# Two places instead of three for weight blocks, three kept query blocks instead of two, in a one-core kernel of a hybrid block

## The chip, the cores and the metric

The kernel runs on one core of a Trainium2 chip. A core has TensorE (PE, matmuls; PEld is its weight load), VectorE (DVE), ScalarE (ACT), GpSimd (POOL) and SyncE (SP), which each run a program of their own in order and meet at semaphores, and 16 DMA engines that move data between HBM and the on-chip memory. The metric is the time of one execution on the device, in microseconds; less is better. A measurement of this kernel tells about 0.2% (3.5 us) from no change.

## The reference

Two layers over 256 tokens of width 1024, in float32. Each layer adds three things to `x`: a mixer (causal convolution, stick-breaking attention and a diagonal state-space model side by side, then `w_out`), cross attention over 256 memory rows (`w_mq`, `w_mkv`, `w_mo`), and a feed-forward layer (PEER) in which each token picks 16 of 16384 experts for each of 8 heads:

```python
def one_chunk(xc):                                   # 128 tokens
    q = (xc @ w_q).reshape(PEER_CHUNK, PEER_HEADS, 2, PEER_HALF)
    sc = jnp.einsum('chid,hikd->chik', q, sub_keys)
    top_s, top_i = lax.top_k(sc, PEER_TOPK)
    cand = (top_s[:, :, 0, :, None] + top_s[:, :, 1, None, :]).reshape(...)
    best_s, best_c = lax.top_k(cand, PEER_TOPK)
    i1 = jnp.take_along_axis(top_i[:, :, 0], best_c // PEER_TOPK, axis=-1)
    i2 = jnp.take_along_axis(top_i[:, :, 1], best_c % PEER_TOPK, axis=-1)
    gate = jax.nn.softmax(best_s, axis=-1)
    u_e, v_e = u_tab[i1 * PEER_KEYS + i2], v_tab[i1 * PEER_KEYS + i2]
    act = jax.nn.gelu(jnp.einsum('chkd,cd->chk', u_e, xc))
    return jnp.einsum('chk,chkd->cd', gate * act, v_e)
```

The gathers of `u_e` and `v_e` are the bulk of the bytes: 2 layers x 256 tokens x 128 experts x 8 KB = 537 MB.

## The kernel before, in words

**Chunks.** The 256 tokens are two chunks of 128; with two layers there are four chunks in turn, 0 to 3 (`ci`; chunks 0 and 1 are layer 0). For each chunk the kernel computes mixer, memory attention and PEER queries; the PEER gathers of a chunk run beside the mixer and the memory attention of the next.

**Gathers.** The 512 gathers (`NG`) each bring the row pair `u_e`, `v_e` of one expert per token, 128 x 2048 floats or 1 MB, into one of nine tiles `slots` (POOL, L962). VectorE forms the dot product with the token (`dot_of`, L1774), ACT the gelu (L1315), VectorE the coefficient, and then either TensorE adds the row through a diagonal matrix (`add_expert`, L851; ACT writes the diagonal, L1302) or VectorE adds it to `x` (`add_slot`); `TAKER` says who. Then the slot is free and POOL issues the gather nine further on.

**Weight blocks.** All weights come in blocks of 1 MB (128 x 2048 floats). Their names (`LIN`): `u`, `val`, `gate`, `q`, `k`, `v` for the mixer; `mk` and `mv`, four each, once a layer for the memory's keys and values; `out`, `mq`, `mo`, four each; `wq`, eight, one for each head of the PEER queries. SP issues the loads (L918) in the order in which TensorE takes the blocks (`take`). `place` says where a block lies: places 0 to 2 are the tile `ring`; places 3 to 9 are slots 2 to 8, used for weights only until the gathers need them (the first `EARLY` = 35 blocks go round all `WIDE` = 10 places, shifted by `AHEAD` = 5); after that blocks go round the three ring places. Places 10 and 11 are the tile `kept`: the first two of a layer's eight `wq` blocks stay there from the first chunk of the layer to the second, which therefore loads only six. The last two are the scratch tiles `W_` and `pr_`, for `u` and `val` of chunk 1. A load waits until the block that lay in its place before is used (`lain`, `free_at`). The first gather into a slot waits for the last block that lay in it.

**Order of the work.** Each engine's program is written out by a clock of ticks: one tick is one gather from tick 100 (`G0`) on. A piece of work (a strand) yields the tick at which its next part stands in the program; within an engine all is in that fixed order, and whatever waits holds up what stands behind it. `WQ_AT` are the ticks of the `wq` blocks, `KEYS_AT` those of the quarters of `mk` and `mv` blocks (3 ticks a block in layer 1), `MIX_AT` those of the halves of the mixer's nine blocks. In layer 1 the `mv` blocks end where chunk 2's mixer begins, so for three ticks both strands use blocks in turn.

**The first gathers.** The route of head 0 of chunk 0 (`routes`, VectorE) gives the first eight experts' indices before the rest. Its softmax is started by ACT in `gates`, at tick 98; the engine has one table of functions loaded at a time, so an `Exp` after a `Sqrt`, or a `Gelu` after an `Exp`, is preceded by a table load (ACT_TABLE_LOAD).

Of the kernel before, what the change touches and what calls it, by code (L numbers as in the profile page):

```python
# [11 lines left out]
ACT = mybir.ActivationFunctionType  # L12
# [19 lines left out]
PH, NK, TOP = 8, 128, 16  # L32
# [20 lines left out]
NPRM = _at  # L53
NVEC = PRM["b"][0]

RING = 3

EARLY = 35
WIDE = 10

AHEAD = 5

STAY = 2
SLOTS = 9
DIAGS = 4
WARM = 3
# [68 lines left out]
def build(nc, x_d, mem_d, blocks_d, prm_d, rows_d, experts_d, out_d):  # L135
    ctx = ExitStack()
    with ctx:
# [207 lines left out]

        def place(ci, what):

            if 0 <= what - FIRST["wq"] < STAY:
                return WIDE + what - FIRST["wq"]
            if ci == 1 and what < 2:  # L350
                return WIDE + STAY + what
            r = sum(p < WIDE for p, _ in spots)
            return (r + AHEAD) % WIDE if r < EARLY else (r - EARLY) % RING

        def lain(j):

            p, n = spots[j]
            return spots.index((p, n - 1)) if n else None

        def home(p):  # L360
            if p < RING:
                return ring[:, p, :]
            if p < WIDE:
                return slots[:, p - RING + 2, :]
            if p < WIDE + STAY:
                return kept[:, p - WIDE, :]
            return (W_, pr_)[p - WIDE - STAY][:, 0:KT * BW]

# [559 lines left out]
        @block.gpsimd  # L928
        def _(eng):
            nc.gpsimd.memset(epsb[:, :], EPS).then_inc(const_ok, 1)  # L930
            nc.gpsimd.memset(onec[:, :], 1.0).then_inc(const_ok, 1)
            nc.gpsimd.memset(zero[:, :], 0.0).then_inc(const_ok, 1)
            nc.gpsimd.memset(ident[:, :], 0.0).then_inc(const_ok, 1)
            nc.gpsimd.memset(ident16[:, :], 0.0).then_inc(const_ok, 1)
            nc.gpsimd.memset(mask[:, :], 0.0).then_inc(const_ok, 1)
            nc.gpsimd.iota(times[:, :], pattern=[[1, TP]], base=0, channel_multiplier=0,
                           allow_small_or_imprecise_dtypes=True).then_inc(const_ok, 1)
            nc.gpsimd.iota(iota16[:, :], pattern=[[1, TOP]], base=0, channel_multiplier=0,
                           allow_small_or_imprecise_dtypes=True).then_inc(const_ok, 1)
            eng.wait_ge(const_ok, 8)  # L940
            nc.gpsimd.affine_select(out=ident16[:, :], in_=ident16[:, :], compare_op=ALU.not_equal, fill=1.0,
                                    base=0, pattern=[[-1, P]], channel_multiplier=1).then_inc(const_ok, 1)
            nc.gpsimd.affine_select(out=ident[:, :], in_=ident[:, :], compare_op=ALU.not_equal, fill=1.0,
                                    base=0, pattern=[[-1, P]], channel_multiplier=1).then_inc(const_ok, 1)
            nc.gpsimd.affine_select(out=mask[:, :], in_=mask[:, :], compare_op=ALU.is_gt, fill=-BIG,
                                    base=0, pattern=[[-1, P]], channel_multiplier=1).then_inc(const_ok, 1)
            for n in range(NG):
                q, k = divmod(n, TOP)

                if k == 0:  # L950
                    eng.wait_ge(idx_ready, q + 2 if q else 1)
                elif n == 8:
                    eng.wait_ge(idx_ready, 2)
                if n >= SLOTS:
                    before = n - SLOTS
                elif n >= 2:

                    done, count = free_at[max(j for j in range(len(order)) if spots[j][0] == RING + n - 2)]
                    eng.wait_ge(done, count)
                if n >= SLOTS:  # L960
                    eng.wait_ge(slot_used if TAKER[before] == "tensor" else slot_added, TAKEN[before] + 1)
                nc.gpsimd.indirect_dma_start(  # L962
                    slots[:, n % SLOTS, :], None, experts_d,
                    bass.IndirectOffsetOnAxis(ap=idx[q % 2][:, k:k + 1], axis=0),
                ).then_inc(arrived[n % SLOTS], 16)

        @block.scalar
        def _(eng):
# [202 lines left out]
            def feed(ci):  # L1171
# [10 lines left out]
                if ci == 0:  # L1182
# [9 lines left out]
                    for i, part in enumerate("ab"):  # L1192
# [3 lines left out]
                        name = ("keys " + part, 0, 0)  # L1196
                        done(act(scores[:, 0, i * NK:(i + 1) * NK], full(name)[:, i * NK:(i + 1) * NK], ACT.Copy), name)
                    root_of_x(0, True)
                else:
                    for i in range(2):  # L1200
                        yield at + LATER[ci] + 88
# [66 lines left out]

            def gates():
                for q in range(NST * PH):  # L1270
                    yield route_tick(q, BEST_OP) + (1 if q else 4)
                    j = q % 2
                    eng.wait_ge(best_ready, q + 1)
                    if q < PH:
                        act(gexp[:, j, :], best[:, j, :], ACT.Exp, scale=rs0[:, :], bias=nbest[:, j, :],
                            accum_out=gsum[:, j, :]).then_inc(gexp_ready, 1)
                    else:
                        act(gexp[:, j, :], best[:, j, :], ACT.Exp, bias=nbest[:, j, :], accum_out=gsum[:, j, :])\
                            .then_inc(gexp_ready, 1)
# [661 lines left out]
```

## Time and profile before

| | |
|---|---|
| median of 3 runs | 1732.26 us (1731.23 to 1733.24) |
| the profiled execution | 1731.45 us, span 1729.5 us |
| granted TensorE clock | 0.987 of full speed, mean |
| PE busy | 1584.8 us (92%) |
| DVE busy | 1213.5 us (70%) |
| ACT, POOL busy | 601.3 us (35%), 589.0 us (34%) |
| DMA | 680.38 MB, mean 393 GB/s; gathers 536.90 MB, loads from SP 142.24 MB |
| chain that ended last | PE 35%, DMA 32%, DVE 13%, ACT 4% of the span |
| loads of weight blocks | ring 96, slots 26, kept 4, scratch tiles 2: 128 of 1 MB |

A busy PE is not PE at its peak, since ends of matmuls are modelled. Idle time of an engine costs nothing by itself; what counts is what the chain of waits passes through. An instruction's "releaser" is the one whose semaphore ended its wait.

### The profile page before, as it was taken

Reading aid. Unit: us, or ns where it says so; the run is one execution under the profiler, and the core shown is the slowest. Engines: PE = TensorE matmul, PEld = TensorE weight load, DVE = VectorE, ACT = ScalarE, POOL = GpSimd, SP = SyncE. Lnnn points to the kernel's source line nnn. Section 1 sums busy time; section 2 is a strip of 40 time slices with the busy share of each in tenths; the row PEclk is TensorE's granted clock in tenths of the full one; section 3 lists DMA queues with packets and bytes.
Section 4 is the critical chain, followed back from the end, with each engine's and each line's share of the span. In section 5 each row is a group of like instructions: output and inputs, shape, how many; then the busy total and the mean of one; then the engine's idle time right before and its main releaser. Section 6 shows DMA issues by size and latency. Waiting matters only on the chain.

```text
span 1729.5 us, 19577 instructions
## 1 busy us (share of the span) xinstructions
PE 1584.8 (92%) x6594; PEld 959.1 (55%) x6594; DVE 1213.5 (70%) x3359; ACT 601.3 (35%) x1450; POOL 589.0 (34%) x527
## 2 busy tenths in 40 slices
PE   8999989998999999998999989999999988777776
PEld 7877866445557776644646547644655643222232
DVE  7730689985896667997557567898657577667665
ACT  4133431553345132255223242255323223222222
POOL 0000153443334323344334343344333444333431
PEclk9999999999999999999999999999999999999999
DMA  9636799999999999999999999999999999999996
GB/s 383 245 150 239 292 392 421 421 405 421 421 407 412 421 421 420 420 421 421 421 422 420 421 419 421 419 368 402 422 421 421 421 421 421 421 421 421 420 421 258
DMA packets 94579, 680.38 MB, mean 393 GB/s; under 512 B 10488, under 2 KB 10768, under 8 KB 12304
## 3 DMA queue, kind: packets, MB, share of 16 engines
q0 software_dynamic: 73728, 536.90, 75.3%
q1 hardware_dynamic: 20752, 142.24, 20.2%
q8 instruction: 52, 0.85, 0.2%
q14 instruction: 47, 0.39, 0.1%
HBM read 678.06 MB, written 1.05 MB: 393 GB/s over the span
## 4 chain that ended last, share of the span: by engine, by line
PE 35%; DMA 32%; DVE 13%; ACT 4%; issue 2%; POOL 0%; DVEq 0%; ACTq 0%
DMA slots<-expert_rows,expert 32%; PE bank L851 20%; PE bank L408 7%; DVE slots L1774 5%; PE bank L586 2%; PE bank L839 2%; PE bank L836 2%; ACT diag L1302 1%; DVE sg L1341 1%; DVE htok L1625 1%; PE bank L453 1%; DVE coef L1341 1%; DVE x L1341 1%; DVE cands L1755 0%; ACT L1315 0%
## 5 line engine op out<-in xcount | busy, mean ns | idle before, releaser
L851 PE MATMUL bank<-slots,diag 128*128 128x512 f32 x1916 | 909.6, 611 | 128.9 <-ACT diag L1302 123.8
L962 POOL DMA_INDIRECT slots<-expert_rows,expert x512 | 587.0, 1147 | 1115.5 <-PE bank L851 856.7
L1774 DVE CUSTOM_DVE_ANT_0 slots<-slots,htok 128x1024 f32<-128x1024 f32 x512 | 626.6, 1224 | 336.6 <-DMA slots<-expert_rows,expert 323.5
L851 PEld LDWEIGHTS bank<-slots,diag 128*128 128x128 f32 x1916 | 348.6, 193 | 544.7 <-issue 324.2
L1315 ACT ACTIVATE gel<-dot 128x2 f32<-128x2 f32 (+1 forms) x258 | 52.5, 204 | 675.6 <-DVE dot L1774 674.8
L1302 ACT ACTIVATE diag<-ident,coef 128x128 f32<-128x128 f32 x479 | 168.2, 394 | 190.4 <-DVE coef L1341 181.8
L408 PEld LDWEIGHTS bank<-hT,ring 128*128 128x128 f32 x1632 | 198.6, 193 | 44.7 <-issue 44.4
L408 PE MATMUL bank<-hT,ring 128*128 128x128 f32 x1632 | 199.0, 276 | 0.0
L1341 DVE SCALAR_TENSOR_TENSOR coef<-gel,ginv,gexp 128x2 f32<-128x2 f32 (+1 forms) x258 | 55.1, 213 | 58.6 <-ACT gel L1315 57.1
L1315 ACT ACT_TABLE_LOAD x66 | 84.7, 1283 | 1.2
L1341 DVE SCALAR_TENSOR_TENSOR sg<-pad,prm,sg 128x128 f32<-128x128 f32 x240 | 71.7, 344 | 0.0
L408 PE MATMUL bank<-hT,slots 128*128 128x128 f32 x480 | 56.7, 276 | 3.7 <-DMA slots<-w_blocks 2.5
L408 PEld LDWEIGHTS bank<-hT,slots 128*128 128x128 f32 x480 | 55.2, 192 | 5.1 <-DMA slots<-w_blocks 2.7
L586 PE MATMUL bank<-ring,products 128*128 128x512 f32 x120 | 57.1, 603 | 0.0
L586 PE MATMUL bank<-ring,hT 128*128 128x512 f32 x112 | 52.3, 593 | 0.0
L1774 DVE DVE_READ_ACCUMULATOR2_ANT dot<- 128x1 f32 x512 | 42.3, 83 | 0.0
L1341 DVE SCALAR_TENSOR_TENSOR x<-slots,coef,x 128x1024 f32<-128x1024 f32 x33 | 42.2, 1280 | 0.0
L586 PEld LDWEIGHTS bank<-ring,products 128*128 128x128 f32 x120 | 23.0, 195 | 27.0 <-issue 26.9
L586 PEld LDWEIGHTS bank<-ring,hT 128*128 128x128 f32 x112 | 21.0, 190 | 23.8 <-issue 23.6
L839 PE MATMUL bank<-ring,w 128*128 128x256 f32 x128 | 29.3, 379 | 0.0
L836 PE MATMUL bank<-w,ring 128*128 128x256 f32 x128 | 29.1, 379 | 0.0
L408 PEld LDWEIGHTS bank<-hT,kept 128*128 128x128 f32 x208 | 25.2, 192 | 5.7 <-issue 5.7
(315 smaller groups left out, 1520.4 us busy)
## 6 DMA issues: line engine op xcount, KB each, us to landing
ring<-w_blocks SPq DMA_DIRECT2D x96, 1024.0 KB
slots<-w_blocks SPq DMA_DIRECT2D x26, 1024.0 KB, 7.2
slots<-expert_rows,expert POOLq DMA_INDIRECT x512
kept<-w_blocks SPq DMA_DIRECT2D x4, 1024.0 KB, 12.9
keys<-w_blocks SPq DMA_DIRECT2D x2, 1024.0 KB, 10.7
prm<-small SPq DMA_DIRECT2D x2, 768.0 KB
x<-x_rows SPq DMA_DIRECT2D x2, 512.0 KB, 11.6
slots<-mem_rows SPq DMA_DIRECT2D x1, 1024.0 KB, 9.1
```

The lines of the kernel that those rows point to most:

```text
L408: last = mm(bank[b][:, a * P:(a + 1) * P], w[:, k, a * P:(a + 1) * P], src[:, k, :], start=k == 0, stop=k == KT - 1)
L453: last = mm(bank[b][:, 0:BW], hT[:, k, :], w[:, k, :], start=k == 0, stop=k == KT - 1)
L586: last = mm(bank[b + i][:, :], src[:, first + k, :], w[:, k, i * 512:(i + 1) * 512], start=start and k == 0, stop=stop and k == 1)
L836: last = mm(bank[b][:, a * M:(a + 1) * M], w[:, k, a * P:(a + 1) * P], memH[l][:, k, :], start=k == 0, stop=k == KT - 1)
L839: last = mm(bank[b][:, a * BW:(a + 1) * BW], memH[l][:, k, a * P:(a + 1) * P], w[:, k, :], start=k == 0, stop=k == KT - 1)
L851: last = mm(bank[h][:, :], diag[:, i % DIAGS, :], slots[:, n % SLOTS, D + h * 512:D + (h + 1) * 512], start=m == 0, stop=n == end)
L962: nc.gpsimd.indirect_dma_start(slots[:, n % SLOTS, :], None, experts_d, bass.IndirectOffsetOnAxis(ap=idx[q % 2][:, k:k + 1], axis=0),).the ...
L1302: act(diag[:, i % DIAGS, :], ident[:, :], ACT.Copy, scale=coef[:, q % 2, k:k + 1])\
L1315: act(gel[:, q % 2, k:k + many], dot[:, q % 2, k:k + many], ACT.Gelu_apprx_tanh).then_inc(gelu_ready, 1)
L1341: return v.scalar_tensor_tensor(out=out, in0=in0, scalar=scalar, in1=in1, op0=op0, op1=op1)
L1625: did(v.tensor_tensor_scan(back(stay[:, h, lo:S]), back(sn[:, h, lo:S]), zero[:, :].to_broadcast([P, S - lo]), 1.0, ALU.mult, ALU.add))
L1774: v.tensor_tensor_reduce(out=slots[:, s, 0:D], in0=slots[:, s, 0:D], in1=htok[:, ph % 2, :], scale=1.0, scalar=0.0, op0=ALU.mult, op1=ALU.add,
```

## The change

The tile `ring` has two places instead of three and `kept` three instead of two, so both together take the same memory. The kept blocks are now the last three of a layer's `wq` blocks (heads 5 to 7) instead of the first two. The wide round has nine places, ring 0 and 1 and the seven slots, of which the first 34 blocks use; `slot_at` maps place 2 to slot 6, 3 to 7, 4 to 8, and 5 to 8 to slots 2 to 5. With the new `EARLY` and `AHEAD`, chunk 0's `wq` blocks 0 and 1 lie in the ring, 2 to 4 in slots 6 to 8, 5 to 7 in `kept`, and its four `mo` blocks in slots 2 to 5. Before, its `wq` blocks 0 and 1 lay in `kept` and 2 to 7 in slots 3 to 8, and its last `mo` block in slot 2. The second chunk of each layer loads five `wq` blocks instead of six: 126 loads instead of 128. Besides, ACT executes one more `Exp` of a zero in the opening, whose table load comes earlier, and the softmax of head 0 of chunk 0 stands at tick 94 of ACT's program instead of 98.

```diff
-RING = 3
+RING = 2
-EARLY = 35
-WIDE = 10
-AHEAD = 5
-STAY = 2
+EARLY = 34
+WIDE = 9
+AHEAD = 7
+STAY = 3
...
         def place(ci, what):
-            if 0 <= what - FIRST["wq"] < STAY:
-                return WIDE + what - FIRST["wq"]
+            if what >= FIRST["wq"] + PH - STAY:
+                return WIDE + what - (FIRST["wq"] + PH - STAY)
...
+        def slot_at(p):
+            return 2 + (p - RING + 4) % (WIDE - RING)
+
         def home(p):
             if p < RING:
                 return ring[:, p, :]
             if p < WIDE:
-                return slots[:, p - RING + 2, :]
+                return slots[:, slot_at(p), :]
...
-                    done, count = free_at[max(j for j in range(len(order)) if spots[j][0] == RING + n - 2)]
+                    done, count = free_at[max(j for j in range(len(order))
+                                              if RING <= spots[j][0] < WIDE and slot_at(spots[j][0]) == n)]
...
                     root_of_x(0, True)
+                    act(ahead[:, :], zero[:, :], ACT.Exp)
...
-                    yield route_tick(q, BEST_OP) + (1 if q else 4)
+                    yield route_tick(q, BEST_OP) + (1 if q else 0)
```

POOL's program at the first gathers (slots 0 to 8 in turn, then slot 0 again), before. `filled` and `pair_used` are TensorE's signals that a block has been used, `slot_used` and `slot_added` that an expert has been added, `idx_ready` that indices are there:

```order
L962 DMA slots<-expert_rows,expert 128x2048 [waits idx_ready]
L962 DMA slots<-expert_rows,expert 128x2048
L962 DMA slots<-expert_rows,expert 128x2048 [waits filled3] x2
L962 DMA slots<-expert_rows,expert 128x2048 [waits filled2]
L962 DMA slots<-expert_rows,expert 128x2048 [waits filled3]
L962 DMA slots<-expert_rows,expert 128x2048 [waits filled2]
L962 DMA slots<-expert_rows,expert 128x2048 [waits filled3]
L962 DMA slots<-expert_rows,expert 128x2048 [waits filled2,idx_ready]
L962 DMA slots<-expert_rows,expert 128x2048 [waits slot_used] x2
```

and now:

```order
L967 DMA slots<-expert_rows,expert 128x2048 [waits idx_ready]
L967 DMA slots<-expert_rows,expert 128x2048
L967 DMA slots<-expert_rows,expert 128x2048 [waits pair_used] x3
L967 DMA slots<-expert_rows,expert 128x2048 [waits filled3] x2
L967 DMA slots<-expert_rows,expert 128x2048 [waits filled2]
L967 DMA slots<-expert_rows,expert 128x2048 [waits filled3,idx_ready]
L967 DMA slots<-expert_rows,expert 128x2048 [waits slot_used] x2
L967 DMA slots<-expert_rows,expert 128x2048 [waits slot_added]
```

Slots 2 to 4 now wait for `mo` blocks (`pair_used`), slot 5 for the last of them, and slots 6 to 8 for `wq` blocks 2 to 4; before, six gathers waited for `wq` blocks 2 to 7.

ACT's program around the first softmax (`gexp`), before; `qT` holds the queries of a head, L1219 copies them out of a bank, L1210 the scores:

```order
L993 ACTIVATE root<-ss,epsb 128x1 [waits act_step]
L1219 ACTIVATE qT<-bank 128x256 [waits filled2]
L1210 ACTIVATE scores<-bank 128x256 [waits filled5]
L1219 ACTIVATE qT<-bank 128x256 [waits filled3]
L1210 ACTIVATE scores<-bank 128x256 [waits filled6]
L1219 ACTIVATE qT<-bank 128x256 [waits filled2]
L1275 ACT_TABLE_LOAD
L1275 ACTIVATE gexp,gsum<-best,nbest,rs 128x16 [waits best_ready]
L1210 ACTIVATE scores<-bank 128x256 [waits filled5]
L1219 ACTIVATE qT<-bank 128x256 [waits filled3]
```

and now:

```order
L998 ACTIVATE root<-ss,epsb 128x1 [waits act_step]
L1204 ACT_TABLE_LOAD
L1204 ACTIVATE ahead<-zero 128x1
L1225 ACTIVATE qT<-bank 128x256 [waits filled2]
L1281 ACTIVATE gexp,gsum<-best,nbest,rs 128x16 [waits best_ready]
L1216 ACTIVATE scores<-bank 128x256 [waits filled5]
L1225 ACTIVATE qT<-bank 128x256 [waits filled3]
L1216 ACTIVATE scores<-bank 128x256 [waits filled6]
L1225 ACTIVATE qT<-bank 128x256 [waits filled2]
L1216 ACTIVATE scores<-bank 128x256 [waits filled5]
```

The softmax stands behind one copy of queries instead of three, and its table load before the copy of head 1's queries; the first `gel` (not shown) has the same five copies of queries ahead of it in both.

TensorE's program where the last `mv` blocks (L839, now L843) and chunk 2's first blocks `u`, `val`, `gate` (L408, now L412) meet, before; `loaded0` to `loaded2` are the loads into the ring's places:

```order
L839 MATMUL bank<-ring,w 128x256 x4
L408 MATMUL bank<-hT,ring 128x128 [waits loaded2,emptied2,emptied5]
...
L839 MATMUL bank<-ring,w 128x256 [waits loaded0,emptied4]
L839 MATMUL bank<-ring,w 128x256 x7
...
L408 MATMUL bank<-hT,ring 128x128 x8
L839 MATMUL bank<-ring,w 128x256 x4
...
L408 MATMUL bank<-hT,ring 128x128 [waits loaded1,emptied3]
L408 MATMUL bank<-hT,ring 128x128 x7
L839 MATMUL bank<-ring,w 128x256 x4
L408 MATMUL bank<-hT,ring 128x128 x8
...
L408 MATMUL bank<-hT,ring 128x128 [waits loaded2,emptied2]
```

and now:

```order
L843 MATMUL bank<-ring,w 128x256 x4
L412 MATMUL bank<-hT,ring 128x128 [waits loaded1,emptied2,emptied5]
...
L843 MATMUL bank<-ring,w 128x256 [waits loaded0,emptied4]
L843 MATMUL bank<-ring,w 128x256 x7
...
L412 MATMUL bank<-hT,ring 128x128 x8
L843 MATMUL bank<-ring,w 128x256 x4
...
L412 MATMUL bank<-hT,ring 128x128 [waits loaded1,emptied3]
L412 MATMUL bank<-hT,ring 128x128 x7
L843 MATMUL bank<-ring,w 128x256 x4
L412 MATMUL bank<-hT,ring 128x128 x8
...
L412 MATMUL bank<-hT,ring 128x128 [waits loaded0,emptied2]
```

The instructions are the same and stand in the same order. What moved is the place: `u` waits for place 1 instead of 2, the last `mv` block for place 0, which the third `mv` block leaves in this piece's first row, `val` for place 1, which `u` leaves two instructions earlier, and `gate` for place 0, which the last `mv` block leaves between the halves of `val`.

## Rows read from the trace of the kernel before

**Rows 1.** Stages: span, busy us (instructions) of PE, PEld, DVE, ACT, POOL; PEclk, DMA share, GB/s

```profile
210.00:220.00 10.00, 8.81 (x57) 6.73 (x56) 6.61 (x15) 7.90 (x15) 2.96 (x4) 1.00 0.50 168
...
476.00:545.00 69.00, 66.14 (x307) 42.07 (x306) 52.02 (x142) 34.31 (x78) 24.55 (x21) 0.95 1.00 406
545.00:676.00 131.00, 131.00 (x650) 100.47 (x649) 90.09 (x223) 39.59 (x92) 45.97 (x39) 1.00 1.01 421
676.00:1120.00 444.00, 416.22 (x1725) 246.24 (x1724) 321.27 (x900) 149.42 (x371) 168.34 (x142) 0.98 1.01 420
1120.00:1200.00 80.00, 75.08 (x258) 36.69 (x257) 73.26 (x194) 46.28 (x92) 34.12 (x27) 1.00 0.98 381
1200.00:1690.00 490.00, 414.60 (x1310) 204.71 (x1309) 325.77 (x891) 143.75 (x381) 196.52 (x184) 0.99 1.01 421
```

**Rows 2.** Chain of waits around 664 us: start, us, what

```profile
663.88 20.35 DMA slots<-expert_rows,expert
```

**Rows 3.** Timeline of POOL, opening: start, us, engine, line, what, [idle before <-releaser]

```profile
188.74 1.09 POOL L962 DMA_INDIRECT slots<-expert_rows,expert  x1 [186.07 <-DVE expert L1341]
...
193.24 0.94 POOL L962 DMA_INDIRECT slots<-expert_rows,expert  x1 [0.82 <-PE bank L408]
...
200.32 0.94 POOL L962 DMA_INDIRECT slots<-expert_rows,expert  x1 [3.08 <-PE bank L408]
...
216.32 0.94 POOL L962 DMA_INDIRECT slots<-expert_rows,expert  x1 [6.18 <-PE bank L408]
```

**Rows 4.** Timeline of ACT, then VectorE, opening

```profile
196.47 1.28 ACT L1275 ACT_TABLE_LOAD   x1
197.76 0.40 ACT L1275 ACTIVATE gexp<-best,nbest,rs 128x16 f32<-128x16 f32 x1
...
198.35 0.16 DVE L1781 RECIPROCAL ginv<-gsum 128x1 f32<-128x1 f32 x1 [2.82 <-ACT gexp L1275]
...
206.04 0.22 DVE L1341 SCALAR_TENSOR_TENSOR coef<-gel,ginv,gexp 128x2 f32<-128x2 f32 x1 [3.30 <-ACT gel L1315]
```

**Rows 5.** Waits of VectorE 224 to 256, of TensorE 224 to 300: us, times, longest

```profile
DVE slots L1774 <- DMA slots<-expert_rows,expert: 3.5, 5, 1.0
...
PE bank L851 <- ACT diag L1302: 3.4, 2, 2.1
```

**Rows 6.** DMA issues of 164, 605 and 871 us: KB each, us from issue to landing

```profile
w<-w_blocks SPq DMA_DIRECT2D x1, 1024.0 KB, 4.8
...
keys<-w_blocks SPq DMA_DIRECT2D x1, 1024.0 KB, 14.5
...
kept<-w_blocks SPq DMA_DIRECT2D x2, 1024.0 KB, 16.1
```

**Rows 7.** Timeline of SP's queue around the stretch of mk and mv

```profile
605.06 0.33 SPq L918 DMA_DIRECT2D ring<-w_blocks  x1
...
615.40 0.33 SPq L918 DMA_DIRECT2D ring<-w_blocks  x1
```

**Rows 8.** Timeline of TensorE at the out blocks of chunk 1

```profile
371.66 3.60 PE L586 MATMUL bank<-ring,hT 128*128 128x512 f32 x8
...
380.25 1.88 PE L586 MATMUL bank<-ring,hT 128*128 128x512 f32 x4
```

**Rows 9.** Timeline of TensorE where mv's last blocks and chunk 2's first meet

```profile
635.95 1.89 PE L839 MATMUL bank<-ring,w 128*128 128x256 f32 x8
...
639.46 3.62 PE L839 MATMUL bank<-ring,w 128*128 128x256 f32 x16
...
644.63 1.95 PE L408 MATMUL bank<-hT,ring 128*128 128x128 f32 x16
...
649.86 1.95 PE L408 MATMUL bank<-hT,ring 128*128 128x128 f32 x16
651.64 1.89 PE L839 MATMUL bank<-ring,w 128*128 128x256 f32 x8
...
658.16 3.73 PE L408 MATMUL bank<-hT,ring 128*128 128x128 f32 x32
```

## The prediction

> **What bounds the kernel now.** I read the table of stages first. The DMA engines move 421, 420 and 421 GB/s from 545 to 676, 676 to 1120 and 1200 to 1690 us, but 406 from 476 to 545 and 381 from 1120 to 1200 [rows 1]. A block of weights and a gather are 1.05 MB each (128 rows of 8 KB), so each costs 1.05 / 421 = 2.49 us of that throughput. Two engines stand close behind: TensorE is busy 131.00 of 131.00 us from 545 to 676 us, and VectorE 73.26 of 80.00 us from 1120 to 1200 us [rows 1]. So DMA is full, but the end passes through DMA only where the engines have slack; elsewhere a megabyte saved becomes idle DMA.
>
> Then the chain of waits. It runs through TensorE's instructions up to 663.6 us and at 663.88 goes over to one gather that is 20.35 us from issue to landing [rows 2]: 8 MB stand in the queues, some 5 or 6 gathers and the weight blocks. That backlog is what a TensorE stall can eat before DMA goes idle.
>
> **The change part by part.** *The opening's gathers.* POOL issues the first gather at 188.74 us, and its fourth to ninth at 193.24 to 216.32 us, most held by query blocks that TensorE still reads in slots 3 to 8 (the ninth waits 6.18 us for the last of them); DMA falls to 168 GB/s between 210 and 220 us [rows 1, 3]. In the changed kernel slots 2 to 5 hold mo blocks, done before 177 us, slots 6 to 8 the third to fifth query blocks. At POOL's own spacing of 1.24 to 1.4 us six gathers go out by 195 us, and the ninth when the fifth query block is done: today that is what releases the sixth gather, 200.32 us [rows 3]. The ninth is 16 us earlier, and DMA, which needs 2.49 us for each, is some 7 us further by 225 us. Of this, 2.5 us go again, because chunk 1's fifth block can no longer be fetched before the gathers start. What the engines can make of the 5 us left is less. The first coefficients wait for ACT until 206.04 us, and ACT's place in its program is behind query blocks that TensorE computes until 208 us, so nothing before 206 moves [rows 4]. From 224 us on VectorE waits for gathers 3.5 us in all, five times, the longest 1.0 us, and TensorE for diagonals 3.4 us, in two waits of which the longest is 2.1 us, its only ones until 300 us [rows 5]. So the gain lies between 0 (the waits turn into others) and 5 us (DMA's whole lead). I take 3, what the rows of waits give.
>
> *The exp edits.* They take a table load of 1.28 us and the wait of 2.82 us out of VectorE's way at 198.35 us [rows 4]. VectorE today then waits 3.30 us for the first gelu, at 206.04, and that wait grows by what the other loses. I cost this at 0; the cover is ACT's order behind the query copies. If that cover were gone it would be worth up to 2.8 us. The Trainium skill, page "ScalarE: Activation LUTs", section "What ACT_TABLE_LOAD costs", puts a drain of 1380 ns behind the 1283 ns of the load. The trace disagrees on the drain: the exp starts 1.29 us after its load started [rows 4]. By the page the edit would free 2.66 us, still under the same cover.
>
> *Two blocks less to load.* Three kept query blocks instead of two save one load in the second chunk of each layer: 2 x 2.49 = 5.0 us of DMA. The first saving falls near 486 to 545 us, the stage in which DMA has idle time already (406 GB/s) and which TensorE, busy 66.14 of 69 and then 131 of 131, carries on [rows 1]: worth nearly nothing. The second falls into 1200 to 1690, where DMA is full; but with a ring of two each load is issued one block later, so one block more is still to come when this stage begins at about 1195 us, and 12 loads are issued in it then as now. Bounds 0 and 5.0 us, I take 1.
>
> *Ring of two: which blocks come late.* With two places a block is issued when the block before the last is done, and has to land while one block is used. What a load takes: 4.8 us with no gather under way; 14.5 us for the keys issued 0.8 us behind a weight block, so two megabytes among gathers; 16.1 us for the kept pair behind a third [rows 6]. A single one among gathers therefore needs between 4.8 and 14.5 us; I take 9 (estimate: half of 14.5 is 7.3, a third of 16.1 is 5.4, and both carry the gathers ahead of them once more). Going through all uses, the time from one block's end to the start of the next but one is over 10 us almost everywhere: in the mk and mv stretch loads leave 10.3 us apart [rows 7], so a block has 10.3 us plus the gap between two. It is less in these places:
> - The out block used fourth, in chunks 1, 2 and 3: the instructions from 371.66 to 375.26 us are the second out block's last half and the third's first, so the second ends at about 373.5, and the fourth is used at 380.25 [rows 8]: 6.8 us, short by 2.2. Three of these make 6.6 us of TensorE stall. At 380 us two weight blocks and three or more gathers are under way, over 10 us of DMA work, so little reaches the end: between 0 and 6.6, I take 1.
> - The seam of layer 1's mv blocks and chunk 2's u, where both strands use blocks at once. Mv's third block ends at 637.84 and its fourth starts at 639.46: gap 1.6. U ends at 646.58, val starts at 649.86: 3.3. The fourth mv block ends at 653.5, gate starts at 658.16: 4.6 [rows 9]. At 9 us each the stalls are 7.4, 5.7 and 4.4: 17.5 us in which TensorE, the busiest engine there, stands. While it stands, no add of experts frees a slot, gathers under way dwindle, and loads get quicker; with the second and third load at 7 us the sum is 7.4 + 3.7 + 2.4 = 13.5.
>
> What these 13.5 us cost: the gather that is issued at 663.88 today and lands at 684.2 [rows 2] is issued at 677.4 and then finds nearly empty queues. Alone it would need about 5 us, with the weight blocks asked for in the same moments 10: it lands at 682 to 687. So the end is between 0 (the backlog of 20.35 us swallows all) and 17.5 + 10 - 20.35 = 7.2 us later; I take 3.
>
> Everything queued behind a waiting TensorE instruction (adds, then slots, POOL's gathers, then VectorE's dot products) is in that account. On SP's queue chunk 2's kept loads now leave as three in a row with the fourth-to-last query load, a burst of 4 MB; DMA stays full and TensorE has 28 us of slack in that stage (416.22 of 444 [rows 1]), so 0. Opening blocks in nine instead of ten places: each is issued over 30 us before its use, 0.
>
> **The sum.** -3 (opening) - 0 (exp) - 1 (bytes) + 1 (out) + 3 (seam) = 0. The profiled execution took 1731.45 us with a span of 1729.5; the median of the runs is 1732.26, 0.8 above it. I forecast the same time, 1732.3.
>
> **Rivals.**
> - *A, faster: DMA decides throughout.* For it: 420 and 421 GB/s in stages that make up 1065 of the 1729.5 us [rows 1]. Then the lead of 5 us in the opening and the 5.0 us of the two blocks arrive whole, and the stalls vanish in the backlog: -5 - 5 + 1 = -9, 1723. Against it: TensorE's 131 of 131 us, and the two stages in which DMA idles. Half of it, -5 (1727), is what comes if only one of the savings arrives. Chance 0.31 for all that is faster by over 0.2%.
> - *B, slower: the seam stalls TensorE past the backlog.* One mechanism at one place, 637 to 680 us: the loads stay at 9 us or more, or the gathers' issue comes back later than I count. With 17.5 us of stall and a gather that needs 10 us after it, +7.2; with the opening at 0 to -3 the sum is +5 to +8, so 1737 to 1740. It decides from some 17 us of stall on: 17 + 10 - 20.35 = 6.6, and the other terms (-3 - 1 + 1) leave +3.6. Chance 0.25. The Trainium skill, page "DMA: Bandwidth & Descriptors", section "Queues, rings and completion order", says that each DMA engine takes turns between the queues that have work, a packet at a time. By that rule a weight block's landing does not get shorter until the gathers are all but gone, so the stalls would be the 17.5 us of B and not 13.5. The kept pair's 16.1 us for loads issued among gathers [rows 6] don't contradict it, and no row here shows a load with only one gather beside it.
> - *C, the change does not do what it says:* the earlier gathers bring nothing, since query blocks, ACT and VectorE set the pace until 254 us. Then +3 on my sum, 1735: still within 0.2%. It is part of the 0.44 for no change.
>
> **Chances and range.** 0.2% is 3.5 us, about what a measurement of this kernel tells from no change. My forecast with C: 0.44; A 0.31; B 0.25. The range of 8 in 10 reaches into A to 1725 (the half case and some) and into B to 1740. The forecast's own range is 1729 to 1735.5.
>
> **What would show it.** Opening: the ninth gather issued at about 200 us instead of 216.32, DMA above 300 GB/s between 210 and 220, VectorE's waits for gathers before 256 gone. The exp: no wait for gexp at 198 us, the first coefficients still at about 206 us. Ring: TensorE waiting for loads of weights at the fourth out block by 2 us and at the start of mv's last block, val and gate by 7, 4 and 2, nowhere else by more than 1; DMA's throughput between 640 and 690 below 421. Loads: 126 weight blocks instead of 128. I am wrong if the seam shows under 5 us or over 17 us of stall, if the shift at 300 us is not -1 to -5, or if the shift from 700 us to the end changes by more than 2.

## The result, and the profile after

The changed kernel takes 1741.47 us (median of 5 runs, 1738.5 to 1742.34) where the kernel before takes 1732.9 (1731.23 to 1733.44): the ratio is 1.0055, with a 95% interval of 1.0043 to 1.0067. That is slower, and outside the range of 1725 to 1740. The profiled execution took 1741.47 us with a span of 1739.5.

Of the page of the changed kernel these lines answer to the ones of before: the engines' busy shares, the granted clock and DMA's throughput in 40 slices, two groups on TensorE that now wait for weight blocks, and the loads.

```profile
span 1739.5 us, 19572 instructions
PE 1588.9 (91%) x6594; PEld 963.5 (55%) x6594; DVE 1211.6 (70%) x3359; ACT 601.3 (35%) x1451; POOL 580.6 (33%) x527
...
GB/s 385 216 149 262 295 368 422 409 411 411 421 421 420 421 395 295 421 421 421 421 421 421 421 421 420 421 385 399 417 421 421 421 421 422 421 421 422 421 421 275
...
L590 PE MATMUL bank<-ring,hT 128*128 128x512 f32 x96 | 49.2, 643 | 7.9 <-DMA ring<-w_blocks 7.9
...
L843 PE MATMUL bank<-ring,w 128*128 128x256 f32 x128 | 33.5, 418 | 7.6 <-DMA ring<-w_blocks 7.6
...
ring<-w_blocks SPq DMA_DIRECT2D x92, 1024.0 KB
slots<-w_blocks SPq DMA_DIRECT2D x26, 1024.0 KB, 6.8
...
kept<-w_blocks SPq DMA_DIRECT2D x6, 1024.0 KB, 12.4
```

The slices are 43.5 us long. The 16th, 652 to 696 us, moves 295 GB/s, the least between 218 us and the last slice, and the one ahead of it 395. The table of stages (columns as in [rows 1]) puts it more finely.

```profile
210.00:220.00 10.00, 10.00 (x69) 8.09 (x68) 8.08 (x23) 7.12 (x16) 2.18 (x3) 1.00 0.79 303
...
545.00:676.00 131.00, 120.14 (x541) 91.37 (x539) 74.85 (x176) 31.34 (x78) 36.72 (x32) 0.93 0.92 377
640.00:646.00 6.00, 0.39 (x4) 0.20 (x2) 4.85 (x13) 0.40 (x1) 0.00 (x0) 0.80 1.02 423
646.00:654.00 8.00, 5.98 (x15) 4.77 (x16) 0.05 (x1) 0.00 (x0) 0.00 (x0) 0.51 0.45 188
654.00:660.00 6.00, 6.00 (x32) 4.62 (x31) 0.00 (x0) 0.38 (x1) 0.94 (x1) 1.00 0.30 79
660.00:664.00 4.00, 1.52 (x4) 0.38 (x2) 0.00 (x0) 0.00 (x0) 1.88 (x2) 1.00 1.04 424
664.00:671.00 7.00, 6.25 (x23) 5.74 (x24) 0.00 (x0) 0.00 (x0) 0.00 (x0) 0.51 0.74 291
...
1200.00:1690.00 490.00, 416.85 (x1305) 205.39 (x1304) 330.30 (x909) 143.95 (x381) 195.97 (x184) 0.99 1.01 420
```

From 646 to 660 us DMA falls to 188 and 79 GB/s, VectorE does next to nothing until 671, and TensorE works at a granted clock of 0.51 in two of the stretches. TensorE's timeline there, against [rows 9]:

```profile
636.72 1.89 PE L843 MATMUL bank<-ring,w 128*128 128x256 f32 x8
638.44 1.95 PE L412 MATMUL bank<-hT,ring 128*128 128x128 f32 x16
648.02 6.56 PE L843 MATMUL bank<-ring,w 128*128 128x256 f32 x16 [7.63 <-DMA ring<-w_blocks]
654.42 1.88 PE L855 MATMUL bank<-slots,diag 128*128 128x512 f32 x4
656.13 1.95 PE L412 MATMUL bank<-hT,ring 128*128 128x128 f32 x16
...
664.75 3.75 PE L412 MATMUL bank<-hT,ring 128*128 128x128 f32 x16 [3.23 <-DMA ring<-w_blocks]
668.30 3.18 PE L843 MATMUL bank<-ring,w 128*128 128x256 f32 x8
671.32 1.95 PE L412 MATMUL bank<-hT,ring 128*128 128x128 f32 x16
...
676.42 3.81 PE L412 MATMUL bank<-hT,ring 128*128 128x128 f32 x32 [0.16 <-DMA ring<-w_blocks]
```

Gate's block starts at 676.42 instead of 658.16. Of these 18.3 us, 7.63 + 3.23 + 0.16 = 11.0 are waits. Another 6.0 are the same matmuls at half clock: 6.56 for 3.62, 3.75 for 1.95, 3.18 for 1.89. The chain of waits runs through exactly these pieces:

```profile
638.63 9.25 DMA ring<-w_blocks
...
648.02 6.56 PE bank L843 x16
...
658.11 6.51 DMA ring<-w_blocks
...
664.75 3.75 PE bank L412 x16
...
671.51 4.77 DMA ring<-w_blocks
```

Val's load is issued at 658.11, 19.5 us after the mv block's: it waits for the end of u, whose second half (656.13) stands behind the mv block on TensorE. With u ending at 646.58, as in [rows 9], it would have been 8.

What each engine waited for from 636 to 700 us (us in total, times, longest):

```profile
POOL slots L967 <- PE bank L855: 47.1, 9, 17.2
DVE coef L1347 <- ACT gel L1321: 26.2, 1, 26.2
ACT memV L1266 <- PE bank L843: 18.0, 2, 13.0
ACT uT L1033 <- PE bank L412: 17.4, 1, 17.4
```

This is how a wait on TensorE spreads: ScalarE stands 17.4 us at the copy of u and 13.0 at the copy of mv, the gelu behind them comes late, VectorE stands 26.2 us at one coefficient (longest before: 5.5), no slot is freed, and POOL issues no gather for 17.2 us.

To see where time goes over the whole run I compare the start of VectorE's dot product n (L1774, now L1780; the first is 0) in pairs of traces; dot product n needs gather n. Us later than in the trace of before:

```
n                  1    8    32    56    64    88   136   144   160   208   240   312   320   384   448
changed kernel   -1.7 +4.9 +0.9  +1.3  +5.7   0.0  -2.2 +17.9 +12.1 +11.8 +18.0 +11.8 +15.0 +10.1 +10.0
e_mv3_kept       -0.6 +4.1 +0.1  +0.5  +6.7  +2.1  +1.2  +5.6  +0.4  +0.4  +6.7  +0.5  +5.9  +0.6  +0.7
e_busy_short     -2.3 +0.1 -1.2  -0.8  +4.6  -1.3  -2.0 +12.2  +6.7  +5.9 +12.1  +5.9  +9.6  +4.6  +4.6
e_ring2_alone    +3.7 +3.7 +5.6  +4.3 +11.6  +5.4  +6.4 +22.7 +17.4 +16.1 +16.1 +16.1 +20.9 +18.2 +18.2
```

The last column is the end. The first gather itself is issued 1.0, 2.2, 0.1 and 3.7 us later than before in these traces, by how the first weight loads land within 20 us of the start; that offset has to be taken off before one reads a term. In the changed kernel all of the loss is made between 136 and 160 (+14.3); the steps at 64, 240 and 320 are given back. A trace is one execution and need not be its kernel's median: that of e_mv3_kept took 1732.24 us (median 1727.53), that of e_busy_short 1736.0 (1732.69) and that of e_ring2_alone 1749.76 (1747.1), each the slowest of its kernel's runs. So I read steps between two n from the traces, and totals from the medians.

### The profile page after: what moved, and what is told of

It reads as the page before. It is cut to its first block, busy times and chain, and to the rows that moved or that the text cites. A ratio compares the mean times of both kernels' runs of the same rounds, so it can differ in the third digit from the quotient of the medians.

```text
span 1739.5 us, 19572 instructions
## 1 busy us (share of the span) xinstructions
PE 1588.9 (91%) x6594; PEld 963.5 (55%) x6594; DVE 1211.6 (70%) x3359; ACT 601.3 (35%) x1451; POOL 580.6 (33%) x527
## 4 chain that ended last, share of the span: by engine, by line
PE 53%; DMA 29%; DVE 8%; issue 5%; ACT 4%; SPq 0%; POOL 0%; DVEq 0%
DMA slots<-expert_rows,expert 25%; PE bank L855 24%; PE bank L412 10%; PE bank L590 4%; DMA ring<-w_blocks 3%; PE bank L843 3%; DVE slots L1780 3%; PE bank L840 3%; PE bank L457 1%; PE bank L490 1%; ACT diag L1308 1%; PE bank L475 1%; DMA slots<-w_blocks 1%; PE bank L678 1%; PE bank L420 1%
## 5 line engine op out<-in xcount | busy, mean ns | idle before, releaser
L967 POOL DMA_INDIRECT slots<-expert_rows,expert x512 | 578.7, 1130 | 1133.9 <-PE bank L855 888.8
L1780 DVE CUSTOM_DVE_ANT_0 slots<-slots,htok 128x1024 f32<-128x1024 f32 x512 | 625.6, 1222 | 279.6 <-DMA slots<-expert_rows,expert 269.7
L412 PEld LDWEIGHTS bank<-hT,ring 128*128 128x128 f32 x1584 | 192.8, 193 | 48.8 <-issue 47.6
L412 PE MATMUL bank<-hT,ring 128*128 128x128 f32 x1584 | 194.3, 277 | 5.2 <-DMA ring<-w_blocks 4.4
L412 PEld LDWEIGHTS bank<-hT,kept 128*128 128x128 f32 x384 | 45.9, 192 | 8.1 <-issue 8.1
L412 PE MATMUL bank<-hT,slots 128*128 128x128 f32 x352 | 43.6, 281 | 6.2 <-DMA slots<-w_blocks 4.5
L412 PE MATMUL bank<-hT,kept 128*128 128x128 f32 x384 | 46.3, 275 | 0.0
L412 PEld LDWEIGHTS bank<-hT,slots 128*128 128x128 f32 x352 | 42.1, 197 | 7.3 <-issue 3.7
L590 PE MATMUL bank<-ring,products 128*128 128x512 f32 x96 | 45.1, 592 | 0.0
L1780 DVE DVE_READ_ACCUMULATOR2_ANT dot<- 128x1 f32 x512 | 41.8, 82 | 0.0
L843 PE MATMUL bank<-ring,w 128*128 128x256 f32 x128 | 33.5, 418 | 7.6 <-DMA ring<-w_blocks 7.6
L843 PEld LDWEIGHTS bank<-ring,w 128*128 128x128 f32 x128 | 27.0, 214 | 14.7 <-issue 10.7
## 6 DMA issues: line engine op xcount, KB each, us to landing
keys<-w_blocks SPq DMA_DIRECT2D x2, 1024.0 KB, 11.8
```

Of the source, the lines that this page charges most:

```text
L412: last = mm(bank[b][:, a * P:(a + 1) * P], w[:, k, a * P:(a + 1) * P], src[:, k, :], start=k == 0, stop=k == KT - 1)
L590: last = mm(bank[b + i][:, :], src[:, first + k, :], w[:, k, i * 512:(i + 1) * 512], start=start and k == 0, stop=stop and k == 1)
L843: last = mm(bank[b][:, a * BW:(a + 1) * BW], memH[l][:, k, a * P:(a + 1) * P], w[:, k, :], start=k == 0, stop=k == KT - 1)
L967: nc.gpsimd.indirect_dma_start(slots[:, n % SLOTS, :], None, experts_d, bass.IndirectOffsetOnAxis(ap=idx[q % 2][:, k:k + 1], axis=0),).the ...
L1780: v.tensor_tensor_reduce(out=slots[:, s, 0:D], in0=slots[:, s, 0:D], in1=htok[:, ph % 2, :], scale=1.0, scalar=0.0, op0=ALU.mult, op1=ALU.add,
```

## The experiments

Each was timed beside the kernel before, on the same chip. The times are medians; the ratio to before, given with its 95% interval, is not the quotient of the two medians.

**e_ring2_alone: the ring of two and nothing else.** The kernel before with

```diff
-RING = 3
+RING = 2
...
-WIDE = 10
-
-AHEAD = 5
+WIDE = 9
+
+AHEAD = 1
```

> The kernel before with a ring of two places and nothing else of the change: two kept query blocks, the opening's query blocks in slots 3 to 8, exp and gates as before. Theory (the seam): the whole loss is made where layer 1's last mv block, val and gate are waited for, about 14 us between VectorE's 136th and 160th dot product, and the bytes saved by the third kept block gave about 4 us of it back in the changed kernel. So this one should be slower than the changed kernel: 1732.9 + 14 = 1747 us (1745 to 1749). Rival (the bytes are worth nothing, as the prediction had it at 1 us, and part of the loss comes from the opening or the out blocks): 1741 to 1743 us. In the profile the theory wants TensorE waits of 7 to 8 us and 3 us for ring blocks at 640 to 665 us, and the granted clock at its lower level behind them.

Measured: 1747.1 us against 1732.73, ratio 1.0074 (1.0057 to 1.009). TensorE's waits for weight blocks in it:

```profile
PE bank L586 <- DMA ring<-w_blocks: 9.6, 3, 4.1
PE bank L839 <- DMA ring<-w_blocks: 7.4, 1, 7.4
PE bank L408 <- DMA ring<-w_blocks: 5.3, 3, 3.1
...
PE bank L836 <- DMA ring<-w_blocks: 2.8, 1, 2.8
```

The time is as the theory had it, and the rest of the change is worth 5.6 us of gain. The clock is not as the theory had it: in the seam it falls behind the first wait alone, and for a shorter time.

```profile
656.50 5.93 PE L839 MATMUL bank<-ring,w 128*128 128x256 f32 x16 [7.43 <-DMA ring<-w_blocks]
...
672.49 2.02 PE L408 MATMUL bank<-hT,ring 128*128 128x128 f32 x16 [3.11 <-DMA ring<-w_blocks]
```

That is 2.4 us of half clock instead of 6.0, and the step between dot products 136 and 160 is 11.0 us instead of 14.3. A mk block (L836) waits too, which no mk block does in the changed kernel. Of the other 7.2 us at the end of this trace 3.7 are there from the start and 2.5 come between n = 376 and 384, of which more below (e_ring2_mv3).

**e_mv3_kept: one block out of the ring.** The changed kernel with, in `place`,

```diff
+            if ci == 2 and what == FIRST["mv"] + 3:
+                return WIDE
```

> The changed kernel with one block moved out of the ring: layer 1's last mv block goes into a kept place, which is empty between chunk 1's and chunk 2's query blocks. Theory: one wait starts it all. Val's and gate's waits follow from the first, since u's second half stands behind the mv block on TensorE and the loads of val and gate wait for u and mv; with it all three go, the clock stays up, and the time is 1741.5 - 14 = 1727.5 us (1726.5 to 1729), 0.3% below the kernel before. Rival (each of the three waits stands by itself, as the prediction summed them): val's and gate's waits of 3 to 4 us each stay and the time is 1732 to 1737 us.

Measured: 1727.53 us, ratio 0.9964 (0.9951 to 0.9977): the 14 us go, and the kernel is faster than before. In the traces the step between 136 and 160 goes from +14.3 to -0.8. TensorE there:

```profile
644.96 3.69 PE L845 MATMUL bank<-kept,w 128*128 128x256 f32 x16 [1.14 <-DMA kept<-w_blocks]
...
655.44 1.95 PE L414 MATMUL bank<-hT,ring 128*128 128x128 f32 x16
```

Val (655.44) no longer waits: its load goes out when the third mv block is done, and gate's when u is. So the three waits were one chain with one start. Moving one block is enough.

**e_busy_wait and e_busy_short: the same waits, with TensorE busy.** The changed kernel with matmuls whose result is overwritten, ahead of the wait for the mv block and for val:

```diff
+            def idle_turns(b, many):
+                for _ in range(many):
+                    mm(bank[b][:, 0:BW], ident[:, :], T[:, 0, :, 0:P], start=True, stop=True)
...
+                                if (kind, i, l) == ("mv", 3, 1):
+                                    idle_turns(b, 34)
...
+                    if (n, ci) == (1, 2):
+                        idle_turns(b, 14)
```

> The changed kernel with matmuls whose result nobody reads placed on TensorE ahead of the two waits: 34 of 128x256 ahead of the last mv block (about 7.3 us) and 14 ahead of val (about 3.0 us). The loads come when they come, so the waits are no shorter, but TensorE is busy in them. Theory: of the 18 us by which TensorE is late at gate's block, 6 us are matmuls at the granted clock of 0.5 behind the two waits (the mv block took 6.56 us instead of 3.62, val's first half 3.75 instead of 1.95, the next mv half-block 3.18 instead of 1.89). With the clock kept up 6 us go, and at the end 4 to 6 us: 1735.5 to 1737.5 us. Rival (the clock does not matter there, because DMA or VectorE sets the pace, or the fall has another cause): 1741 to 1743 us.

Measured: 1745.6 us, ratio 1.0081 (1.0067 to 1.0096). A miss: one matmul of this kind stands as two instructions in the trace, and I had taken the duration of one instruction for that of a matmul.

```profile
639.95 14.84 PE L410 MATMUL bank<-phasor,ident 128*128 128x256 f32 x68
654.63 3.62 PE L852 MATMUL bank<-ring,w 128*128 128x256 f32 x16
```

The filling is 7.2 + 3.0 us longer than the waits, but the mv block takes 3.62 us again. The second try has `idle_turns(b, 17)` and `idle_turns(b, 7)`.

> The changed kernel with half of the matmuls of the try before: 17 ahead of the last mv block (68 pieces took 14.84 us there, so these take 7.4 us, the length of the wait) and 7 ahead of val (3.1 us). Theory (half clock costs 6 us of the 18): the try before was too long by 7.2 + 3.0 us and ran 4.1 us longer than the changed kernel, which is 10.2 less the 6 us of the clock. With the right length 4 to 6 us go: 1735.5 to 1737.5 us. Rival (the clock does not matter, and the try before only lost less than its length): 1741 to 1743 us.

Measured: 1732.69 us against 1732.74, ratio 1.0001 (0.9992 to 1.001): 8.8 us less than the changed kernel, more than the 4 to 6 expected.

```profile
640.49 7.50 PE L410 MATMUL bank<-phasor,ident 128*128 128x256 f32 x34
648.35 3.72 PE L852 MATMUL bank<-ring,w 128*128 128x256 f32 x16 [0.35 <-DMA ring<-w_blocks]
...
671.02 3.81 PE L417 MATMUL bank<-hT,ring 128*128 128x128 f32 x32 [0.46 <-DMA ring<-w_blocks]
```

The mv block still cannot start before 648.35, and nothing else of the change was touched, yet gate starts at 671.02 instead of 676.42, with the granted clock at 1.00 throughout. Between dot products 136 and 160 this kernel loses 8.7 us and the changed one 14.3. So 5.6 us of the seam is the half clock; e_ring2_alone fits, with 3.6 us less of half clock on TensorE and 3.3 us less of loss. The medians are 8.8 us apart and the two profiled executions 5.5. Where the other 3.2 us of the medians lie no trace shows: the seam may cost more in other executions, or the opening (this trace lacks the stop told below and starts its gathers 0.9 us earlier).

**e_opening: the opening alone.** The kernel before (ring of three, exp as before) with the last two query blocks kept and

```diff
+            if 29 <= r < EARLY:
+                return (0, 1, 7, 8, 9, 2)[r - 29]
```

and `AHEAD = 8`, so that slots 2 to 5 are free early.

> The kernel before with the changed kernel's opening alone: ring of three, two kept blocks, but these are the last two, and the third to fifth query blocks stand in slots 6 to 8, the others in the ring, so that slots 2 to 5 are free for gathers early. Exp and gates as before. The prediction on record gives this -3 us (1730), from gathers that come earlier. Theory now: the first coefficients wait for ScalarE and TensorE, dot products 2 to 9 are no earlier, and by 300 us the shift is 0: 1732 to 1734 us. A third way: the stop of 2.3 us that TensorE shows at 197.5 us in the changed kernel, while nine gathers are asked for at once, belongs to this opening; then a stop of 2 to 3 us shows here at 195 to 200 us too, and dot products 2 to 9 are 3 to 5 us later than before.

Measured: 1729.06 us, ratio 0.9981 (0.9972 to 0.999), so -3.7: the prediction on record was right here, and my theory after the result wrong. I had read the trace of the changed kernel at n = 8 (+4.9), where a stop of TensorE hides the gain; that stop shows here too.

**e_exp_alone: the two edits for exp, in the kernel before.**

```diff
+                    act(ahead[:, :], zero[:, :], ACT.Exp)
...
-                    yield route_tick(q, BEST_OP) + (1 if q else 4)
+                    yield route_tick(q, BEST_OP) + (1 if q else 0)
```

> The kernel before with the two edits for exp alone (the function is called up early, and the first exp's tick is 4 less). The prediction on record and the theory: 0, since the first coefficients wait for ScalarE's order behind the query copies: 1732 to 1734 us. Rival: the earlier exp saves up to 2.8 us on VectorE, 1730.

Measured: 1731.33 us against 1732.74, ratio 0.9997 (0.9988 to 1.0006). No difference that can be told. The wait moves as predicted: the one for gexp is gone, and

```profile
204.77 0.22 DVE L1342 SCALAR_TENSOR_TENSOR coef<-gel,ginv,gexp 128x2 f32<-128x2 f32 x1 [6.02 <-ACT gel L1316]
```

the one for the first gelu has grown from 3.30 to 6.02 us, at the old place (this trace runs 1.3 us ahead from its first loads on).

**e_mv3_reload3: what a load costs.** e_mv3_kept, in which `take` loads the three kept query blocks again for the second chunk of each layer (`and c` becomes `and c > 1`).

> The changed kernel with the mv block in a kept place (1727.5 us), in which the three kept query blocks are loaded again for the second chunk of each layer, into the same places: 132 loads instead of 126, six times 1.05 MB, 15 us of DMA. Nothing else moves. The prediction on record takes 1 us of 5.0 for two loads saved, so 3 us of 15: 1730 to 1731 us. Theory now (a kernel with a ring of two and two kept blocks ran 5.6 us longer than the changed kernel, of which the opening is 3.7, so two loads are worth about 2): 6 us, 1733 to 1734. Rival (each megabyte arrives whole): 15 us, 1742.

Measured: 1739.53 us, ratio 1.0046 (1.0032 to 1.0059): 12.0 us for six loads, 2.0 each. Against e_mv3_kept its dot products go from 1.8 us earlier at n = 352 to 5.6 later at n = 376, where the second layer's three loads lie and DMA moves 421 GB/s: 7.4 us, three times 2.49 whole. Both my theory (6) and the prediction (3, by its 1 of 5.0) were low; the rival, each megabyte whole (15), was nearer.

**e_mv3_spaced: the gathers of the opening spread out.** e_mv3_kept with, on POOL,

```diff
+                    if n == 5:
+                        done, count = free_at[order.index((0, FIRST["wq"] + 3))]
+                        eng.wait_ge(done, count)
```

> The changed kernel with the mv block in a kept place, whose sixth gather waits until the fourth query block is done (about 198.5 us) instead of leaving at 197: five gathers are on their way instead of seven when TensorE came to its stop of about 2 us at 197 to 200 us in all four kernels that ask for nine gathers at once. DMA still has work for 12 us. If the stop comes from the heap of gathers, it is gone or shorter in the profile, dot products 2 to 9 are 2 us earlier against the first gather, and the time is 0 to 2 us less than 1727.5. If it comes from something else at that place of the program (code that is fetched then, say), it is still there at the same matmuls.

Measured: 1726.62 us, ratio 0.9969 (0.9959 to 0.998). TensorE's stop is not in its trace, but the median is only 0.9 below e_mv3_kept, which the measurement does not tell from nothing.

**e_ring2_mv3: the ring of two without its seam.** e_ring2_alone with the same two lines in `place`.

> The kernel before with a ring of two (as the run with the ring of two alone, 1747.1 us), and layer 1's last mv block in a kept place. Opening, kept query blocks and exp as before, 128 loads. Theory: outside the seam a ring of two costs next to nothing, since the waits of 2.5 to 3 us at the fourth out block of three chunks are made up by the gathers on their way; so this is the kernel before again, 1732 to 1735 us. Rival (the out blocks cost what they wait, 6 to 9 us in all, as the upper bound of the prediction had it): 1739 to 1742.

Measured: 1735.34 us against 1733.03, ratio 1.0014 (1.0005 to 1.0023), just above the 1735 of the theory. So outside the seam two places cost 2.3 us. Against e_ring2_alone the one block is worth 11.8 us here (1747.1 less 1735.34) where it was worth 14.0 in the changed kernel. Its trace waits 8.6 us for the three fourth out blocks and gives those back; it loses 2.5 us between n = 376 and 384. The last weight block is asked for at 1376.7 us instead of 1363.5, and so lies among gathers that had DMA for themselves; from 1200 us on this kernel asks for 13 weight blocks, the kernel before for 12.

**e_seam_all_kept: val and gate in kept places too** (`if ci == 2 and 1 <= what < 3: return WIDE + what`, on e_mv3_spaced).

> The kernel with the mv block in a kept place and the sixth gather held back (1726.6 us), with val and gate of chunk 2 in kept places too, so that no block of the seam waits for the ring. TensorE still waits 1.4 us for the mv block and 1.4 us in two waits for val and gate there. Theory: these short waits are made up by the gathers on their way, so nothing is left: 1725.5 to 1727.5 us. Rival (they reach the end): 1724 us.

Measured: 1726.22 us, ratio 0.9966 (0.9952 to 0.998): as the theory had it, and not to be told from e_mv3_spaced or e_mv3_kept.

## Why the prediction was wrong

The sum on record was -3 - 0 - 1 + 1 + 3 = 0. The runs price its terms like this:

- *Opening, -3.* Right: -3.7 (e_opening). DMA moves 303 GB/s from 210 to 220 us instead of 168, and VectorE's waits for gathers before 256 us are gone, as forecast. The shift I wanted to see at 300 us (-1 to -5) did not show in the changed kernel's trace (+0.9 at n = 32, of which 1.0 is the start). The stop of TensorE told below may be a part of that, but is not shown to be all of it: less the start, the shift at n = 32 is -0.1 (changed), -0.6 (e_busy_wait), -2.1 (e_mv3_kept) and -3.1 (e_opening) in traces with the stop, and -1.3 (e_busy_short) and -3.9 (e_mv3_reload3) without. The ninth gather is issued at 205.70 us and not at 200, and at 200.92 in e_busy_short, which has no stop; the first coefficients stand at 210.91 and not at 206.
- *Exp, 0.* Right in time and in mechanism (e_exp_alone).
- *Two loads less, -1.* Mis-sized: about -4 by the price of a load in e_mv3_reload3 (two of six in 12.0 us). The step that failed is that the first saving is "worth nearly nothing". The changed kernel goes from +0.8 at n = 104 to -2.2 at n = 136 (524 to 630 us in the kernel before), and so, by 2.9 to 3.0 us, do all six kernels with two places and three blocks that stay kept; e_ring2_alone and e_ring2_mv3, with two kept blocks, move by +0.3 and +0.2. The step on the second saving, "12 loads are issued in it then as now", held: from 1200 us on e_mv3_kept asks for 12 weight blocks as the kernel before does, and e_ring2_mv3, whose ring of two is not made up by a kept block, for 13, which costs it 2.5 us. So the -4 here and the +2.3 of the next point hold that one load with opposite signs.
- *Out blocks, +1.* Right in mechanism: the wait of TensorE at the fourth out block is 7.9 us in three waits (2.2 each were forecast), and n = 64 and 320 show steps that are gone at 88 and 384. The half clock is here too: the four matmuls behind these waits take 3.61, 2.99 and 3.56 us in the changed kernel, against 1.88 for four at full clock. The burst of kept loads in chunk 2, priced at 0, shows the same way at n = 240 (+18.0) and is gone at 312. With what else two places cost it is +2.3 (e_ring2_mv3).
- *Seam, +3.* This is what failed: 14.0 us (1741.47 less 1727.53). The waits were foreseen well and in sum a little too high (7.4, 3.7 and 2.4 against 7.63, 3.23 and 0.16), and the first load too (9 us against 9.25). Two things were not in the account. First, a TensorE that waits 7.63 us comes back at half clock: 6.0 us more on TensorE, of which 5.6 reach VectorE's dot product 160 (e_busy_short). Second, "the backlog of 20.35 us swallows": this step of the prediction took one gather's time from issue to landing, at 664 us, as cover for the whole. In the trace POOL ends one gather's issue at 639.3 us and the next at 657.5, and DMA moves nothing from 653 to 658 us, so that a single gather (issued at 656.57) is ahead of the next wait. The stop of the gathers is 18 us and not 7.6, because the adds that free slots wait for VectorE and ScalarE, and ScalarE stands in its order behind the copies of u and mv. Without the clock the 11.0 us of waits still cost 8.7; the backlog covered 2.3. The price of the seam is 14.0 us in the changed kernel and 11.8 in the one with the ring of two alone.

The terms priced so give -3.7 - 1.4 - 4 + 2.3 + 14 = +7.2 (with the exp edits at their median, which is no difference that can be told), or +5.0 with the seam at 11.8, against 8.6 measured.

Of the signs set beforehand, the stall at the seam (11.0 us, between 5 and 17) held; the shift at 300 us did not, and from 700 us to the end the shift changed by 2.1 (+12.1 at n = 160, +10.0 at 448), just more than the 2 allowed.

Of the rivals B came true: the seam past the backlog, at the place named, at 1741.5 instead of 1737 to 1740. Its first condition did not: it wanted loads of 9 us and 17.5 us of waits, and 11.0 did it. Its second, that the gathers' issue comes back later than counted, did, for a reason it did not name. The granted clock of 0.51 behind the waits is the lower of its two levels, 1.2 GHz of 2.4; in [rows 1] the whole stage stood at 1.00. The Trainium skill, page "TensorE: Matmul & The Clock Gate", section "HAM oscillation — how this bites in real kernels", says that a wait for DMA between two blocks of work makes the second start throttled, at a price of half the throttled time; this trace agrees (6.56 us for 3.62). The prediction priced its waits without it. Not every wait has this behind it: of the eleven waits of 2.4 to 4.1 us for a load in the traces of the changed kernel and e_ring2_alone, seven are followed by matmuls at half clock and four, one of 3.11 us among them, are not. The rule on turns between queues that B cited (the Trainium skill, "DMA: Bandwidth & Descriptors", "Queues, rings and completion order") is not contradicted: the three loads took 9.25, 6.51 and 4.77 us, and at their issue 4, 1 and no gathers were under way (two more were issued during the second). What I had wrong was that gathers would still be there.

Of A's -9 some 5 come once the one block is out of the ring: e_mv3_kept is 5.2 us faster than before, about -3.7 - 4 + 2.3. That is A's half case; its full account, both savings and the whole lead, no run shows.

## What to carry to other kernels

Price a wait on TensorE as the wait plus, possibly, the work behind it at half clock (always behind the two waits of over 7 us here, often but not always behind those of 2.4 to 4.1), and look which in-order engines copy the result of the waiting instruction: what stands behind those copies is stopped as well, and the backlog covers it only once. Where two strands share a ring, look for the one block that both wait on; here one more place for one block was worth 12 to 14 us. Where DMA is full, a load saved is worth its bytes, unless the same change moves another load into that stage.

## What the runs showed of the hardware

*TensorE stops with nothing to wait for.* In the changed kernel's opening, in the midst of a query block whose weights had landed long before:

```profile
195.06 2.40 PE L412 MATMUL bank<-hT,slots 128*128 128x128 f32 x20
198.35 0.39 PE L412 MATMUL bank<-hT,slots 128*128 128x128 f32 x2 [0.90 <-issue]
199.08 0.27 PE L412 MATMUL bank<-hT,slots 128*128 128x128 f32 x1 [0.33 <-issue]
199.81 2.24 PE L412 MATMUL bank<-hT,slots 128*128 128x128 f32 x9 [0.45 <-issue]
...
200.30 1.12 POOL L967 DMA_INDIRECT slots<-expert_rows,expert  x1 [1.52 <-remote]
```

Six kernels ask for the first seven gathers back to back; the traces of four (changed, e_mv3_kept, e_busy_wait, e_opening) have such a stop of some 2 us between 197 and 200 us, those of e_busy_short and e_mv3_reload3 have none. The kernels that spread the gathers (before, e_ring2_alone, e_exp_alone, e_ring2_mv3, e_mv3_spaced, e_seam_all_kept) have none either. In the changed kernel the clock then falls too: 0.51 from 199.8 to 203 us. So the stop was seen only with the heap of gathers, which does not force it; what it is stays open.

*The start is not the same twice.* The first gather is issued between 1.5 us before and 3.7 us after its time in the trace of before, by the first loads' landing and by whether the clock falls in TensorE's wait of 3 us at 14 us. One trace against one other cannot show a term of 2 us unless this offset is taken off.
